# A decoder step on one core: the norm, the turning of x and the in-projection put into one block

## The chip, the cores and the metric

The kernel runs on one core of a Trainium2 chip. The metric is the device time of one execution in microseconds (us), lower is better. The core has five engines that run their own instruction streams and meet through semaphores: TensorE (PE, matmuls and transposes), VectorE (DVE), ScalarE (ACT), GpSimd (POOL) and SyncE (SP), which here issues all the DMAs.

## The reference, cut to what matters

All is float32. A prompt of 256 tokens and 8 samples of 4 tokens (288 tokens in all) pass one decoder layer with shared weights:

```python
h = rmsnorm(x, norm_mix)                      # 288 x 1024
proj = h @ w_in                               # 1024 x 3848: 1792 columns for RWKV, 2056 for the delta heads
xm = pr + (prev - pr) * mu_shift              # prev: the row before; for a sample's first row state_rwkv_shift
conv = sum(xp[:, j:j + t] * conv_w[j])        # xp: state_gdn_conv (3 rows) ahead of the projected rows
...                                           # RWKV7 and gated-delta recurrences, w_out, residual
x = x + cross_attention(rmsnorm(x), rmsnorm(mem, norm_mem))
x = x + routed_ffn(rmsnorm(x))                # top 4 of 32 experts, 12.6 MB of weights each
y = rmsnorm(x, final_norm)
```

The change touches only the start: `rmsnorm`, the transposed copy of `h`, the first of the projections and the small inputs that they need.

## The kernel before, in words

**Blocks.** The program is a row of blocks. In a block each engine has its own stream, written by hand; between two blocks all engines meet at a barrier. `front` holds two: a first one for the norm, and a second one for the projection and all that is computed from it. Then follow blocks for the recurrences, the read-out, the attention and the experts.

**The first block.** SP issues, in this order, the three parts of x (two of 128 tokens, one of 32: `TILES`), four norm vectors into `g8`, the weights of group 0 (`load_w(sp, 0)`), nine small vectors into the rows of `vrow`, the two states `shr` and `cvr` into `rc`, and the weights of group 1. ACT squares each part with a row sum (L358; the squares themselves go to `h_tm` and are overwritten) and takes the root (L361). DVE takes the reciprocal and scales the part into `h_tm` (L372, L373). PE turns it, 8 transposes a part (L394), one into each PSUM bank. When the third part is turned, DVE copies the even banks into `hT` and ACT the odd ones, times the norm vector (L378, L366). `idle_products` are products of the identity with itself into a bank that nobody reads, 18 of them at the start and 2 ahead of the second and of the third part; they keep PE at work while it would wait. POOL makes only `eps` and `ident` in this block.

**The second block.** PE first turns the small inputs (`turn_inputs`: `vrow` in one transpose, `shr` in 14, `cvr` in 12) into banks 0, 1 and 2, and DVE copies them into `vec`, `sprev` and `cprev`. Then come 31 projected tiles of 128 columns: `project(t)` is 8 products of 128 x 288 into bank 6 or 7 (an f32 product is two instructions). The weights come in groups of two tiles into three buffers, and a buffer's next load is issued when its last tile is projected. ACT empties a projected tile (`empty(t)`) after `turned_ok`, DVE mixes RWKV tiles (`mix(t)`), and between projections PE does the products that the mixed tiles call for (`decay` after tile 3, `rate` after 5, and so on). POOL builds the masks in this block; PE first waits for them in `key_squares`, after tile 7. SP's queue in this block starts with the weights of group 2, then six loads for `tail_in`, then a wait for `turned` and the load of `memx`, which lies over the columns of `rc` that held the states.

Of the kernel before, what the change touches and what calls it, by code (L numbers as in the profile page):

```python
# [19 lines left out]
P = 128  # L20
# [262 lines left out]
def front(nc, a, out, sb, ps, ident, ones, x, g8, eps, m):  # L283

    with ExitStack() as st:
# [9 lines left out]
        row, shr, cvr = rc[0:1 + NB, 0:R_PROJ], rc[0:NB, 0:R_PROJ], rc[0:NB * NJ, R_PROJ:]  # L295
# [13 lines left out]
        vec_in, small_in, tail_in = sem("vec_in"), sem("small_in"), sem("tail_in")  # L309
# [5 lines left out]
        def load_w(eng, g):  # L315
            c0, n = cols[g]
            eng.dma_start(wst[g % NG][:, :, 0:n], w_view[:, :, c0:c0 + n]).then_inc(w_in[g % NG], 16)

        with ExitStack() as s0:
            h_tm = sb(s0, "h_tm", [P, 3, D])  # L320
            x_sq, x_root, x_h, x_turned = (sem(n) for n in ("x_sq", "x_root", "x_h", "x_turned"))
            x_chain = Count(sem("x_chain"))
            with nc.Block() as block:
                @block.sync
                def _(sp):
                    xp = a["x_prompt"][0].rearrange("(i p) d -> i p d", p=P)
                    for i in range(2):
                        sp.dma_start(x[:, i, :], xp[i]).then_inc(x_in[i], 16)
                    sp.dma_start(x[:NS, 2, :], a["x_sample"].rearrange("b t d -> (b t) d")).then_inc(x_in[2], 16)
                    for i, n in enumerate(("norm_mix", "norm_cross", "norm_mem", "norm_ffn")):  # L330
                        sp.dma_start(g8[:, i, :], a[n][0].rearrange("(p c) -> p c", c=KC)).then_inc(small_in, 16)
                    load_w(sp, 0)
                    rows = [("mu_shift", V_MU, 14), ("a0", V_A0, 4), ("k_k", V_KK, 4), ("k_a", V_KA, 4),
                            ("r_k", V_RK, 4), ("lnx_w", V_LW, 4), ("lnx_b", V_LB, 4), ("conv_w", V_CW, 48),
                            ("gdn_norm_w", V_GN, 1)]
                    for name, r0, n in rows:
                        src = a[name][0]
                        src = (src.rearrange("h n -> (h n)") if name == "r_k" else
                               src.rearrange("w n -> (w n)") if name == "conv_w" else src)
                        sp.dma_start(vrow[r0:r0 + n, :], src.rearrange("(r p) -> r p", p=P)).then_inc(vec_in, 16)  # L340
                    sp.dma_start(shr, a["state_rwkv_shift"][0]).then_inc(vec_in, 16)
                    sp.dma_start(cvr, a["state_gdn_conv"][0].rearrange("b j n -> (b j) n")).then_inc(vec_in, 16)
                    load_w(sp, 1)

                @block.gpsimd
                def _(pool):
                    masks.step(pool, nc.gpsimd.memset(eps[:, 0:1], RMS_EPS))
                    masks.step(pool, nc.gpsimd.memset(eps[:, 1:2], GN_EPS))
                    masks.step(pool, nc.gpsimd.memset(ident[:], 1.0))
                    masks.step(pool, nc.gpsimd.affine_select(ident[:], ident[:], [[-1, P]], ALU.is_equal, 0.0, 0, 1))  # L350

                @block.scalar
                def _(act):
                    act.wait_ge(masks.sem, 1)
                    nc.scalar.activation(stat[:, 0, 3:4], eps[:, 0:1], ACT.Sqrt)
                    for i, (_, n) in enumerate(TILES):
                        act.wait_ge(x_in[i], 16)
                        nc.scalar.activation(h_tm[:n, i, :], x[:n, i, :], ACT.Square,  # L358
                                             accum_out=stat[:n, i, 0:1]).then_inc(x_sq, 1)
                        act.wait_ge(x_sq, i + 1)  # L360
                        nc.scalar.activation(stat[:n, i, 1:2], stat[:n, i, 0:1], ACT.Sqrt, bias=eps[:n, 0:1],  # L361
                                             scale=1.0 / D).then_inc(x_root, 1)
                    act.wait_ge(small_in, 64)
                    for c in range(1, KC, 2):
                        act.wait_ge(x_turned, c + 1)
                        nc.scalar.activation(hT[:, c, :], ps[:, c, 0:T], ACT.Copy, scale=g8[:, 0, c:c + 1])  # L366

                @block.vector
                def _(dve):
                    for i, (_, n) in enumerate(TILES):  # L370
                        dve.wait_ge(x_root, i + 1)
                        x_chain.step(dve, nc.vector.reciprocal(stat[:n, i, 2:3], stat[:n, i, 1:2]))  # L372
                        nc.vector.tensor_scalar(h_tm[:n, i, :], x[:n, i, :], stat[:n, i, 2:3], None,  # L373
                                                ALU.mult).then_inc(x_h, 1)
                    dve.wait_ge(small_in, 64)
                    for c in range(0, KC, 2):
                        dve.wait_ge(x_turned, c + 1)
                        nc.vector.tensor_scalar(hT[:, c, :], ps[:, c, 0:T], g8[:, 0, c:c + 1], None, ALU.mult)  # L378

                @block.tensor  # L380
                def _(pe):
                    pe.wait_ge(masks.sem, 4)

                    def idle_products(n):
                        for _ in range(n):
                            nc.tensor.matmul(ps[:, 7, 384:512], ident[:], ident[:], start=True, stop=True)

                    idle_products(18)
                    for i, (t0, n) in enumerate(TILES):
                        if i:  # L390
                            idle_products(2)
                        pe.wait_ge(x_h, i + 1)
                        for c in range(KC):
                            ins = nc.tensor.transpose(ps[:, c, t0:t0 + n], h_tm[:n, i, c::KC], ident[:n, :n])  # L394
                            if i == 2:
                                ins.then_inc(x_turned, 1)
# [43 lines left out]
        with nc.Block() as block:  # L440
            @block.sync
            def _(sp):
                load_w(sp, 2)
# [6 lines left out]
                sp.wait_ge(turned, 3)  # L450
# [17 lines left out]
            def _(pool):  # L468
                def keep(ap, pattern, base, cm):
                    masks.step(pool, nc.gpsimd.affine_select(ap, ap, pattern, ALU.is_ge, 0.0, base, cm))  # L470

                nc.gpsimd.memset(pr[:, :, 0:1], 0.0).then_inc(pads, 1)
# [46 lines left out]
            def _(pe):  # L519
                def project(t):  # L520
                    q = seq[t]
                    if t == 0 or seq[t - 1].group != q.group:
                        pe.wait_ge(w_in[q.group % NG], 16 * (q.group // NG + 1))
                    if t >= 2:
                        pe.wait_ge(ev, t - 1)
                    for c in range(KC):
                        ins = nc.tensor.matmul(ps[:q.n, 6 + t % 2, 0:T], wst[q.group % NG][:, c, q.at:q.at + q.n],  # L527
                                               hT[:, c, :], start=(c == 0), stop=(c == KC - 1))
                    ins.then_inc(prj, 1)

                def turn_inputs():
# [186 lines left out]
            def _(act):  # L718
# [34 lines left out]

                act.wait_ge(turned_ok, 3)
                for t in range(len(seq)):
# [54 lines left out]
                    elif t in (18, 20):  # L810
                        half = (t - 18) // 2
                        act.wait_ge(mem_t, half + 1)
                        for c in range(4 * half, 4 * half + 4):
# [47 lines left out]
            def _(dve):  # L861
# [44 lines left out]
                def products(which):  # L906

                    for name, j, f0, f1 in which:
# [3 lines left out]
                        for h in range(2):  # L912
# [4 lines left out]

                dve.wait_ge(turned, 1)
                nc.vector.tensor_copy(vec[:, :], ps[:, 0, 0:V_ROWS]).then_inc(turned_ok, 1)
                dve.wait_ge(turned, 2)  # L920
                nc.vector.tensor_copy(sprev[:, :, :].rearrange("p i b -> p (i b)"), ps[:, 1, 0:R_TILES * NB]).then_inc(
                    turned_ok, 1)
                dve.wait_ge(turned, 3)
                nc.vector.tensor_copy(cprev[:, :, :].rearrange("p i b -> p (i b)"),
                                      ps[:, 2, 0:C_TILES * NB * NJ]).then_inc(turned_ok, 1)
# [2282 lines left out]
```

## Time and the profile before

| | us |
|---|---|
| median of 3 runs | 1488.66 |
| lowest, highest run | 1487.46, 1493.93 |
| the profiled execution: span from first to last instruction | 1490.3 |
| PE busy in it | 1442.8 |

The profiled execution has no time of its own beside its span. Below, "busy" of PE is the time in which a matmul was under way, which is not the same as work at its peak. The granted clock is given as a share of 2.4 GHz: 1.00 is 2.4 GHz and 0.50 is 1.2 GHz. Times at the left of a row are from the span's start.

### The profile page before, as it was taken

To read this page: it belongs to the slowest core of one execution; us is meant where nothing else is said; L and a number is where in the kernel's file an instruction comes from. 1 tells how busy PE (TensorE), PEld (TensorE's weight loads), DVE (VectorE), ACT (ScalarE), POOL (GpSimd) and SP (SyncE) were. 2 spreads that over 40 slices of the span, in tenths; PEclk is the share of its full clock that TensorE was granted. 3 is DMA by queue.
4 is the path that set the end of the run, shared out by engine and by line. 5 is a ranking of instruction groups with operands and counts; after the bars stand their busy time and mean duration, and the time that the engine had idled before them with its cause. 6 is when DMAs were issued, how large, how long until landed. Compare 5 with 4: busy or idle time off the path is not lost.

```text
span 1490.3 us, 23019 instructions
## 1 busy us (share of the span) xinstructions
PE 1442.8 (97%) x9763; PEld 729.9 (49%) x9763; DVE 499.2 (33%) x994; ACT 216.8 (15%) x500; POOL 59.5 (4%) x103
## 2 busy tenths in 40 slices
PE   9999999999999999999999999999999999999996
PEld 7777788997477463333333333333333333333322
DVE  3585526237115043232242242223224223223213
ACT  3334222331114030000000000000000000000002
POOL 4010201310000000000000000000000000000000
PEclk9999999999999999999999999999999999999999
DMA  6233435105817667999999999999999999999993
GB/s 205 76 113 115 132 97 146 32 4 192 333 57 277 284 289 314 427 429 424 431 432 427 426 432 430 427 426 429 430 432 427 426 432 427 429 426 433 429 428 142
DMA packets 74693, 471.92 MB, mean 317 GB/s; under 512 B 14660, under 2 KB 48155, under 8 KB 58080
## 3 DMA queue, kind: packets, MB, share of 16 engines
q1 hardware_dynamic: 74592, 470.46, 77.0%
q8 instruction: 77, 1.26, 0.3%
q14 instruction: 24, 0.20, 0.0%
HBM read 463.40 MB, written 7.05 MB: 316 GB/s over the span
## 4 chain that ended last, share of the span: by engine, by line
PE 47%; DMA 16%; DVE 1%; ACT 0%; issue 0%; SPq 0%; DVEq 0%
PE ps L2811 22%; PE ps L2848 13%; DMA w<-in_w_e_dram 10%; PE ps L2596 3%; PE ps L2779 3%; DMA wb<-in_w_e_dram 3%; DMA wa<-in_w_e_dram 3%; PE ps L2803 2%; PE ps L2834 1%; PE ps L2600 1%; PE ps L2773 1%; PE ps L2839 1%; PE ps L2748 0%; PE ps L2756 0%; PE ps L2930 0%
## 5 line engine op out<-in xcount | busy, mean ns | idle before, releaser
L3029 DVE TENSOR_SCALAR kvb<-ps 128x512 f32<-128x512 f32 x32 | 22.1, 692 | 614.6 <-PE ps L2811 614.6
L2848 PE MATMUL ps<-w,kvb 128*64 128x512 f32 x640 | 143.1, 596 | 6.0 <-DMA w<-in_w_e_dram 6.0
L2811 PE MATMUL ps<-wb,kvb 128*64 128x512 f32 x480 | 107.5, 601 | 2.2 <-DMA wb<-in_w_e_dram 2.2
L2811 PE MATMUL ps<-wa,kvb 128*64 128x512 f32 x480 | 106.2, 595 | 2.4 <-DMA wa<-in_w_e_dram 2.4
L2811 PE MATMUL ps<-wc,kvb 128*64 128x512 f32 x448 | 100.8, 603 | 2.5 <-DMA wc<-in_w_e_dram 2.5
L2811 PE MATMUL ps<-wd,kvb 128*64 128x512 f32 x448 | 98.7, 593 | 0.0
L2980 ACT ACTIVATE kvb<-kvb 128x512 f32<-128x512 f32 x32 | 20.2, 631 | 499.0 <-DVE kvb L3029 499.0
L3013 DVE TENSOR_TENSOR x<-x,ps 128x1024 f32<-128x1024 f32 x66 | 79.9, 1216 | 32.7 <-PE ps L2779 32.6
L527 PE MATMUL ps<-yT,wkv 128*128 128x288 f32 x352 | 90.4, 415 | 0.0
L2848 PEld LDWEIGHTS ps<-w,kvb 128*64 128x64 f32 x640 | 43.6, 137 | 91.4 <-issue 79.1
L527 PEld LDWEIGHTS ps<-yT,wkv 128*128 128x128 f32 x352 | 67.2, 193 | 20.9 <-issue 2.7
L2779 PE MATMUL ps<-y,gT 64*128 64x512 f32 x264 | 73.4, 638 | 0.8 <-ACT y L2985 0.8
L2811 PEld LDWEIGHTS ps<-wb,kvb 128*64 128x64 f32 x480 | 34.4, 138 | 72.6 <-issue 69.4
L2811 PEld LDWEIGHTS ps<-wa,kvb 128*64 128x64 f32 x480 | 33.3, 137 | 74.1 <-issue 70.0
L2811 PEld LDWEIGHTS ps<-wc,kvb 128*64 128x64 f32 x448 | 31.5, 138 | 70.7 <-issue 67.3
L2596 PE MATMUL ps<-x,eh_tm 128*128 128x256 f32 x256 | 63.8, 392 | 0.3 <-DVE x L2611 0.3
L2811 PEld LDWEIGHTS ps<-wd,kvb 128*64 128x64 f32 x448 | 31.9, 137 | 64.7 <-issue 63.3
L1253 PE MATMUL ps<-wkv,hTm 128*128 128x256 f32 x256 | 57.1, 381 | 3.8 <-ACT kvb L1271 1.5
L2596 PEld LDWEIGHTS ps<-x,eh_tm 128*128 128x128 f32 x256 | 46.0, 189 | 27.6 <-issue 22.2
L2985 ACT ACTIVATE y<-ps 128x512 f32<-128x512 f32 x32 | 19.1, 597 | 246.9 <-PE ps L2848 246.9
L1253 PEld LDWEIGHTS ps<-wkv,hTm 128*128 128x128 f32 x256 | 48.0, 190 | 11.7 <-issue 5.4
L2811 PE MATMUL ps<-w,kvb 128*64 128x512 f32 x192 | 42.4, 594 | 0.6 <-DMA w<-in_w_e_dram 0.6
(647 smaller groups left out, 1706.9 us busy)
## 6 DMA issues: line engine op xcount, KB each, us to landing
w<-in_w_e_dram SPq DMA_DIRECT2D x40, 2048.0 KB, 23.3
wb<-in_w_e_dram SPq DMA_DIRECT2D x15, 4096.0 KB, 29.0
wa<-in_w_e_dram SPq DMA_DIRECT2D x15, 4096.0 KB
wc<-in_w_e_dram SPq DMA_DIRECT2D x14, 4096.0 KB, 27.2
wd<-in_w_e_dram SPq DMA_DIRECT2D x14, 4096.0 KB, 29.8
w<-in_w_e_dram SPq DMA_DIRECT2D x6, 4096.0 KB, 34.3
wa<-in_w_e_dram SPq DMA_DIRECT2D x6, 2048.0 KB, 30.6
wc<-in_w_e_dram SPq DMA_DIRECT2D x6, 2048.0 KB, 30.9
```

The source lines that it names most:

```text
L527: ins = nc.tensor.matmul(ps[:q.n, 6 + t % 2, 0:T], wst[q.group % NG][:, c, q.at:q.at + q.n], hT[:, c, :], start=(c == 0), stop=(c == KC - 1))
L1253: ins = self.nc.tensor.matmul(self.ps[:, 6, DX * i:DX * i + DX], self.hTm[:, c, P * i:P * i + P], self.w[:, n % self.NW, c, :], start=(c = ...
L2596: nc.tensor.matmul(ps[:, b + h, 0:4 * CAP], h_tm[:, i, P * (HK * h + c):P * (HK * h + c) + P], sel[:, i].rearrange("p e t -> p (e t)"), st ...
L2600: ins = nc.tensor.matmul(ps[m:m + CAP, b + j // 2, 0:4 * CAP], hs[r, c, :], sel[r, 2].rearrange("p e t -> p (e t)"), start=False, stop=Tru ...
L2779: ins = nc.tensor.matmul(ps[:, b + half, :], gT[r, i, :], y[r, :], start=True, stop=True)
L2803: ins = nc.tensor.matmul(ps[CAP * half:CAP * half + CAP, g, :], pick[r, half, :], b1[r, s % 2, :], start=True, stop=False)
L2811: ins = nc.tensor.matmul(ps[CAP * half:CAP * half + CAP, g, :], xe[:, h, c, :], wu[h][:, c, c0:c0 + 512], start=False, stop=(h == 1 and c ...
L2848: ins = nc.tensor.matmul(ps[CAP * half:CAP * half + CAP, 2, :], actT[:, c, h, :], wd[:, h, c, 512 * half:512 * half + 512], start=(h == 0 ...
L2980: nc.scalar.activation(th[:, :], hg[:, :], ACT.Tanh, scale=ALPHA / 2).then_inc(th_ok, 1)
L2985: nc.scalar.activation(y[:, :], ps[:, 2, :], ACT.Copy, scale=0.5).then_inc(y_ok, 1)
L3013: nc.vector.tensor_tensor(v, v, w, ALU.add).then_inc(add_ok if done is None else done, 1)
L3029: nc.vector.tensor_scalar(hg[:, :], ps[:, 0, :], LIMIT, None, ALU.min).then_inc(hg_ok, 1)
```

## The change

The first block is gone, and its streams stand at the head of those of the second. With that:

- SP issues the weights of group 0 ahead of the norm vector `norm_mix`; the other three norm vectors go behind the weights of group 1 (their reader, at tile 18, now waits for them itself). The weights of group 2 follow with no block boundary between.
- `h_tm` lies in `kvb` and the squares go to `junk` in `hTm`, so the block needs no memory of its own. The turned chunk c lands in bank (6 + c) % 8 in place of bank c.
- PE does 14 idle products in place of 18, and none between the parts. Tile 0 is projected right after the turning, each of its 8 products waiting for its own chunk of `hT` (`x_kept_by`). `turn_inputs` stands behind tile 0.
- `cvr` and `shr` are loaded under one another into the same columns of `rc` (rows 0 to 23 and 24 to 31), and 14 transposes of 32 rows turn both. POOL clears the 256 columns that `cvr` doesn't fill first, and SP waits for it.
- POOL's masks follow right behind `ident`.

The diff, cut to its core (what is moved without a change is left out):

```diff
-        row, shr, cvr = rc[0:1 + NB, 0:R_PROJ], rc[0:NB, 0:R_PROJ], rc[0:NB * NJ, R_PROJ:]
+        row = rc[0:1 + NB, 0:R_PROJ]
+        prev, cvr, shr = rc[0:NS, 0:R_PROJ], rc[0:NB * NJ, 0:CONV], rc[NB * NJ:NS, 0:R_PROJ]
+        h_tm = m.kvb[:, 0:3 * D].rearrange("p (i d) -> p i d", i=3)
...
-        with ExitStack() as s0:
-            h_tm = sb(s0, "h_tm", [P, 3, D])
...
-            with nc.Block() as block:
...
-                    idle_products(18)
-                    for i, (t0, n) in enumerate(TILES):
-                        if i:
-                            idle_products(2)
...
             def _(sp):
...
+                load_w(sp, 0)
+                sp.dma_start(g8[:, 0, :], a["norm_mix"][0].rearrange("(p c) -> p c", c=KC)).then_inc(mix_in, 16)
...
+                sp.dma_start(cvr, a["state_gdn_conv"][0].rearrange("b j n -> (b j) n")).then_inc(vec_in, 16)
+                sp.wait_ge(cleared, 1)
+                sp.dma_start(shr, a["state_rwkv_shift"][0]).then_inc(vec_in, 16)
+                load_w(sp, 1)
...
-                sp.wait_ge(turned, 3)
+                sp.wait_ge(turned, 2)
...
+                nc.gpsimd.memset(rc[0:NS, CONV:R_PROJ], 0.0).then_inc(cleared, 1)
...
                     for c in range(KC):
+                        if t == 0:
+                            pe.wait_ge(x_kept_by[c % 2], c // 2 + 1)
...
+                def turn_x():
+                    for i, (t0, n) in enumerate(TILES):
+                        pe.wait_ge(x_h, i + 1)
+                        for c in range(KC):
+                            ins = nc.tensor.transpose(ps[:, (6 + c) % 8, t0:t0 + n], h_tm[:n, i, c::KC], ident[:n, :n])
...
                 def turn_inputs():
+                    for done in x_kept_by:
+                        pe.wait_ge(done, KC // 2)
...
-                        ins = nc.tensor.transpose(ps[:, 1, i * NB:(i + 1) * NB], shr[:, i * P:(i + 1) * P],
-                                                  ident[:NB, :NB])
-                    ins.then_inc(turned, 1)
-                    for i in range(C_TILES):
-                        ins = nc.tensor.transpose(ps[:, 2, i * 24:(i + 1) * 24], cvr[:, i * P:(i + 1) * P],
-                                                  ident[:24, :24])
+                        ins = nc.tensor.transpose(ps[:, 1, i * NS:(i + 1) * NS], prev[:, i * P:(i + 1) * P],
+                                                  ident[:NS, :NS])
...
-                turn_inputs()
+                pe.wait_ge(masks.sem, 4)
+                idle_products(14)
+                turn_x()
                 for t in range(len(seq)):
                     project(t)
-                    if t == 3:
+                    if t == 0:
+                        turn_inputs()
+                    elif t == 3:
```

On PE, from the start of `front` on, there stood before (`ps` is PSUM, `ident` the identity, `yT` holds `hT`, `wkv` the weights of group 0; an x is a count):

```order
L386 MATMUL ps<-ident 128x128 x17
L394 MATMUL ps<-ident,h_tm 128x128 [waits in_x_h]
L394 MATMUL ps<-ident,h_tm 128x128 x7
L386 MATMUL ps<-ident 128x128 x2
L394 MATMUL ps<-ident,h_tm 128x32 [waits in_x_h]
L394 MATMUL ps<-ident,h_tm 128x32 x7
L323 UNCONDITIONAL_BRANCH
L518 UNCONDITIONAL_BRANCH [waits barrier_Pool_Activation_PE_DVE_SP_release]
L533 MATMUL ps<-ident,vrow 128x87 [waits in_vec_in]
L535 MATMUL ps<-ident,rc 128x8 x14
L539 MATMUL ps<-ident,rc 128x24 x12
L527 MATMUL ps<-yT,wkv 128x288 [waits in_w_in0]
```

And in the changed kernel, where `h_tm` shows as `kvb`:

```order
L486 MATMUL ps<-ident 128x128 x13
L492 MATMUL ps<-ident,kvb 128x128 [waits in_x_h]
L492 MATMUL ps<-ident,kvb 128x128 x7
L492 MATMUL ps<-ident,kvb 128x32 [waits in_x_h]
L492 MATMUL ps<-ident,kvb 128x32 x7
L480 MATMUL ps<-yT,wkv 128x288 [waits in_x_kept_v,in_w_in0]
L480 MATMUL ps<-yT,wkv 128x288 [waits in_x_kept_a]
L500 MATMUL ps<-ident,vrow 128x87 [waits in_vec_in,in_x_kept_a,in_x_kept_v]
L502 MATMUL ps<-ident,rc 128x32 x14
L480 MATMUL ps<-yT,wkv 128x288 x8
```

The barrier between the turned x and the projection is gone, tile 0 stands ahead of the small inputs, and these are 15 transposes in place of 27.

On SP, behind x, there stood before:

```order
L331 DMA g<-in_norm_mix_dram 128x8
L331 DMA g<-in_norm_cross_dram 128x8
L331 DMA g<-in_norm_mem_dram 128x8
L331 DMA g<-in_norm_ffn_dram 128x8
L317 DMA wkv<-in_w_in_dram 128x8x256
```

And in the changed kernel, where six of the nine rows that load `vrow` are left out, each of the others once:

```order
L322 DMA wkv<-in_w_in_dram 128x8x256
L374 DMA g<-in_norm_mix_dram 128x8
L382 DMA vrow<-in_mu_shift_dram 14x128
L382 DMA vrow<-in_conv_w_dram 48x128
L382 DMA vrow<-in_gdn_norm_w_dram 1x128
L383 DMA rc<-in_state_gdn_conv_dram 24x1536
L385 DMA rc<-in_state_rwkv_shift_dram 8x1792 [waits in_cleared]
L322 DMA stage_c<-in_w_in_dram 128x8x256
L388 DMA g<-in_norm_cross_dram 128x8
```

The first weights moved ahead of the norm vector, and three of the four norm vectors behind the second weights.

## Rows read from the trace of the kernel before

**Rows 1.** Page, parts 1 and 2: busy time, the DMA in 40 slices

```profile
PE 1442.8 (97%) x9763; PEld 729.9 (49%) x9763; DVE 499.2 (33%) x994; ACT 216.8 (15%) x500; POOL 59.5 (4%) x103
...
DMA  6233435105817667999999999999999999999993
```

**Rows 2.** Windows: us, busy time of each engine (rows touching it), TensorE's granted clock, DMA share

```profile
1.73:6.73 5.00, 5.00 (x23) 5.00 (x24) 0.82 (x2) 2.81 (x6) 0.00 (x0) 1.00 0.94 279
6.73:12.04 5.31, 5.31 (x47) 5.08 (x45) 2.56 (x7) 2.51 (x8) 0.00 (x0) 1.00 0.91 273
12.04:13.48 1.44, 0.01 (x1) 0.03 (x1) 1.14 (x3) 1.12 (x3) 0.03 (x1) 1.00 1.07 361
13.48:16.64 3.16, 3.15 (x27) 2.96 (x27) 0.52 (x2) 0.00 (x0) 2.59 (x11) 0.51 0.62 202
16.64:20.38 3.74, 3.74 (x9) 2.74 (x9) 1.75 (x8) 0.00 (x0) 3.13 (x10) 0.50 1.08 298
20.38:26.34 5.96, 5.96 (x26) 4.65 (x26) 2.90 (x15) 0.63 (x4) 5.06 (x14) 1.00 0.49 179
26.34:34.10 7.76, 7.76 (x34) 6.08 (x33) 2.68 (x7) 3.32 (x11) 5.04 (x19) 1.00 0.43 137
402.67:406.08 3.41, 3.13 (x16) 2.38 (x16) 1.98 (x4) 1.39 (x3) 0.00 (x0) 1.00 1.05 400
406.08:412.91 6.83, 6.15 (x14) 4.38 (x14) 0.00 (x0) 3.72 (x7) 0.00 (x0) 0.50 0.89 330
```

**Rows 3.** Timeline of TensorE (PE) from 0 to 140: start us, us, what

```profile
10.98 1.06 PE L394 MATMUL ps<-ident,h_tm 32*128 32x32 f32 x8
13.48 0.33 PE L533 MATMUL ps<-ident,vrow 87*128 87x87 f32 x1 [1.44 <-PEq L323]
13.75 1.66 PE L535 MATMUL ps<-ident,rc 8*128 8x8 f32 x14
15.26 1.45 PE L539 MATMUL ps<-ident,rc 24*128 24x24 f32 x12
16.64 9.86 PE L527 MATMUL ps<-yT,wkv 128*128 128x288 f32 x32
```

**Rows 4.** Timeline of 0 to 70: VectorE (DVE) and ScalarE (ACT) ahead of the projection

```profile
8.97 0.74 DVE L373 TENSOR_SCALAR h_tm<-x,stat 32x1024 f32<-32x1024 f32 x1
...
11.39 1.79 DVE L378 TENSOR_SCALAR yT<-ps,g 128x288 f32<-128x288 f32 x4 [1.68 <-PE ps L394]
11.49 1.68 ACT L366 ACTIVATE yT<-ps,g 128x288 f32<-128x288 f32 x4 [2.73 <-PE ps L394]
```

**Rows 5.** Same timeline: GpSimd (POOL), and one DVE line beside it and alone

```profile
13.45 0.11 POOL L472 MEMSET pr<- 128x4 f32 x1 [11.77 <-POOLq L323]
...
18.15 3.00 POOL L470 TENSOR_SCALAR_AFFINE_SELECT tr<-tr 128x128 f32<-128x128 f32 x7
...
32.23 0.31 POOL L505 MEMSET v_s<- 128x256 f32 x1
32.27 0.44 DVE L948 TENSOR_SCALAR rw<-xm,vec 128x288 f32<-128x288 f32 x1
...
36.14 0.37 DVE L948 TENSOR_SCALAR rw<-xm,vec 128x288 f32<-128x288 f32 x1
```

**Rows 6.** Same timeline: SyncE's DMA issues (SPq), and what waits for the last

```profile
4.07 0.67 SPq L317 DMA_DIRECT2D wkv<-in_w_in_dram  x1
...
17.61 0.43 SPq L449 DMA_DIRECT2D dtb<-in_a_log_dram  x1
...
22.94 0.24 DVE L937 COPY sc<-dtb 128x4 f32<-128x4 f32 x2 [4.33 <-DMA dtb<-in_a_log_dram]
```

**Rows 7.** DMA issues from 4 to 4.7: KB each, us from issue to landing

```profile
wkv<-in_w_in_dram SPq DMA_DIRECT2D x1, 1024.0 KB, 6.2
```

**Rows 8.** Timeline of SyncE, 493 to 600: experts' weights

```profile
567.41 0.35 SPq L2682 DMA_DIRECT2D wa<-in_w_e_dram  x1
```

**Rows 9.** Chain that ended last, 1340 to 1491: start us, us, what

```profile
1415.83 41.03 DMA wb<-in_w_e_dram
```

More of the change, by code:

```diff
@@ L308, in front @@
         x_in = [sem(f"x_in{i}") for i in range(3)]
-        vec_in, small_in, tail_in = sem("vec_in"), sem("small_in"), sem("tail_in")
+        vec_in, mix_in, small_in, tail_in = sem("vec_in"), sem("mix_in"), sem("small_in"), sem("tail_in")
+        x_sq, x_root, x_h, x_turned, cleared = (sem(n) for n in ("x_sq", "x_root", "x_h", "x_turned", "cleared"))
+        x_kept_by = [sem("x_kept_v"), sem("x_kept_a")]
+        x_chain = Count(sem("x_chain"))
         w_in = [sem(f"w_in{i}") for i in range(NG)]
@@ L529, in project, with idle_products @@
                     ins.then_inc(prj, 1)
+                def idle_products(n):
+                    for _ in range(n):
+                        nc.tensor.matmul(ps[:, 5, 384:512], ident[:], ident[:], start=True, stop=True)
+                def turn_x():
[3 more added lines that the diff above has]
+                            ins = nc.tensor.transpose(ps[:, (6 + c) % 8, t0:t0 + n], h_tm[:n, i, c::KC], ident[:n, :n])
+                            if i == 2:
+                                ins.then_inc(x_turned, 1)
                 def turn_inputs():
+                    for done in x_kept_by:
+                        pe.wait_ge(done, KC // 2)
                     pe.wait_ge(vec_in, 16 * 11)
@@ L752, in exps @@
                                              ACT.Exp, scale=s).then_inc(p_ready, 1)
+                act.wait_ge(masks.sem, 1)
+                nc.scalar.activation(stat[:, 0, 3:4], eps[:, 0:1], ACT.Sqrt)
+                for i, (_, n) in enumerate(TILES):
+                    act.wait_ge(x_in[i], 16)
+                    nc.scalar.activation(junk[:n, i % 2, :], x[:n, i, :], ACT.Square,
+                                         accum_out=stat[:n, i, 0:1]).then_inc(x_sq, 1)
+                    act.wait_ge(x_sq, i + 1)
+                    nc.scalar.activation(stat[:n, i, 1:2], stat[:n, i, 0:1], ACT.Sqrt, bias=eps[:n, 0:1],
+                                         scale=1.0 / D).then_inc(x_root, 1)
+                act.wait_ge(mix_in, 16)
+                for c in range(1, KC, 2):
+                    act.wait_ge(x_turned, c + 1)
+                    nc.scalar.activation(hT[:, c, :], ps[:, (6 + c) % 8, 0:T], ACT.Copy,
+                                         scale=g8[:, 0, c:c + 1]).then_inc(x_kept_by[1], 1)
                 act.wait_ge(turned_ok, 3)
@@ L916, in products @@
                                                     f1[r, :, TP:].rearrange("p (i j) t -> p i j t", i=2), ALU.mult)
+                for i, (_, n) in enumerate(TILES):
+                    dve.wait_ge(x_root, i + 1)
+                    x_chain.step(dve, nc.vector.reciprocal(stat[:n, i, 2:3], stat[:n, i, 1:2]))
+                    nc.vector.tensor_scalar(h_tm[:n, i, :], x[:n, i, :], stat[:n, i, 2:3], None, ALU.mult).then_inc(x_h, 1)
+                dve.wait_ge(mix_in, 16)
+                for c in range(0, KC, 2):
+                    dve.wait_ge(x_turned, c + 1)
+                    nc.vector.tensor_scalar(hT[:, c, :], ps[:, (6 + c) % 8, 0:T], g8[:, 0, c:c + 1], None,
+                                            ALU.mult).then_inc(x_kept_by[0], 1)
                 dve.wait_ge(turned, 1)
@@ L920, in _ @@
                 dve.wait_ge(turned, 2)
[L921 to L925, printed above, removed]
+                before = ps[:, 1, 0:R_TILES * NS].rearrange("p (i r) -> p i r", r=NS)
+                nc.vector.tensor_copy(sprev[:, :, :], before[:, :, NB * NJ:NS]).then_inc(turned_ok, 1)
+                nc.vector.tensor_copy(cprev[:, :, :], before[:, 0:C_TILES, 0:NB * NJ]).then_inc(turned_ok, 1)
                 dve.wait_ge(turned_ok, 3)
```

84 lines of the change are left out of this document (19 added, 65 removed).

## The prediction

> **What bounds the kernel now.** I read the page first, then the windows at the start, the timelines of the engines there, and last the chain that ended last. PE is busy for 1442.8 of 1490.3 us and the DMA engines are at nine tenths and more from the 16th slice of 40 on [rows 1]: the experts are bound by their weights, and the last wait of the chain is 41.03 us for such a load at 1415.83 [rows 9]. The change doesn't touch that. But the stream of weights isn't tied to the clock on the wall: its refills are issued as PE frees buffers, the first at 567.41 [rows 8]. If all that is ahead ends 5 us earlier, the stream starts and ends 5 us earlier. So the question is how much earlier PE comes out of the first blocks, and there PE is the engine to look at: from 13.48 on it has no gap up to 34.10 (busy 3.15 of 3.16, then 3.74 of 3.74, 5.96 of 5.96, 7.76 of 7.76) [rows 2]. I fix the point for the sum at the end of tile 1, which is 26.34 now.
>
> Before that point the reader should see four stretches on PE. Turning x ends at 10.98 + 1.06 = 12.04 [rows 3]. Then PE stands idle for 1.44 us until 13.48, while DVE and ACT copy the turned chunks (until 13.18 and 13.17 [rows 4]) and the barrier passes. The small inputs take from 13.48 to 16.64. Tiles 0 and 1 take 9.70 us from 16.64 to 26.34, where the next two tiles take 7.76, in 32 matmuls of 0.243 each. The difference is the clock: it was granted at 1.2 GHz from 13.5 to 20.38, right after the idle stretch, and at 2.4 GHz otherwise [rows 2].
>
> **The change part by part**, against the profiled execution's 1490.3.
>
> *Turning x earlier.* The third part is scaled at 8.97 + 0.74 = 9.71 [rows 4], but PE starts to turn it at 10.98 [rows 3], since 18 idle products, then two more, stand in the way. Of the idle matmuls 23 were under way in the first 5.00 us, 0.217 each; this is twice the later pace, so PE ran at the lower level there, though the column prints 1.00. With 28 in place of 36 they end near 6.73 + 5 x 0.11 = 7.3, before the second part is ready, and the third part is turned from 9.71 to 10.77 at the earliest. Gain 12.04 - 10.77 = 1.27.
>
> *No idle stretch.* The first copied chunk is there before 10.77: the first transpose of the part ends about 0.27 after 9.71 and a copy takes 1.79 / 4 = 0.45 [rows 4]. Two engines give two chunks each 0.45, and PE needs 4 x 0.243 = 0.97 for two, so `x_kept_by` never holds it after the first. Gain 1.44.
>
> *Small inputs.* Now: 3.16. A transpose of 8 rows costs (15.26 - 13.75) / 14 = 0.108, one of 24 rows (16.64 - 15.26) / 12 = 0.115 [rows 3]. One of 32 rows is the third part's: 8 in 1.06, with a tail, so 0.12. 14 x 0.12 + 0.27 = 1.95 for the new order. Gain 1.2. The wait for `x_kept_by` in it is long done.
>
> *Clock.* If PE stays at 2.4 GHz, tiles 0 and 1 take 7.76. Gain 9.70 - 7.76 = 1.94. This is the one uncertain large term. Its bounds: 1.94, and the other way a low stretch that falls wholly on projections costs 6.83 / 2 = 3.4, taking the length of the second one, 406.08 to 412.91 [rows 2], which turns the term to 1.94 - 3.4 = -1.5.
>
> *DVE beside POOL.* POOL was idle for 11.77 us ahead of 13.45; now the masks are built under the norm. The same DVE line took 0.44 beside a POOL memset and 0.37 alone [rows 5]: +0.07 is the near price. The upper bound is that each scaling waits out one of POOL's instructions, 3.00 / 7 = 0.43. Only the third scaling is on the path. I take -0.15, between the two and nearer to the row.
> The Trainium skill speaks against the change here: SBUF — State Buffer, section "Who interferes with whom", has it that a DVE `tensor_scalar` in a two-port mode and GpSimd share an exclusive port pair, and whoever comes second waits for the whole instruction. By that rule the sum would lose 0.43, not 0.15; the trace shows a slowdown of a fifth on one line and no full wait [rows 5].
>
> *DMAs.* Weights of group 0 took 6.2 us from issue at 4.07 [rows 6, 7], so landed at 10.3. They are now issued ahead of four norm vectors; even unmoved they are in time for 10.77. The norm vector that the copies need is issued just behind them, needed at 10; if it took as long as the weights, from about 3 on, it would land at 9.2. The small inputs were in by 13.48 and are needed at 10.77 + 3.9 = 14.7. Weights of group 2 and the six tail loads stood behind the barrier at 13.45; SP's queue now runs on into them, so the last of them, issued at 17.61 before, is issued some 4 us earlier, which covers most of the 4.33 us that DVE waited for it at 22.94 [rows 6]. What is queued behind the new wait for `cleared` (one state, all later loads) doesn't suffer: POOL clears 256 columns right after `ident`, long before SP gets there. I cost all of this at nothing; the cover on the weights is 0.5 us if they aren't earlier at all, and each us beyond it would cost one.
>
> *What is late next.* DVE begins to mix tile 0 some 3 us after the small inputs, which now stand behind tile 0 and not ahead of it. PE first needs a mixed tile in `decay`, after tile 3. It will be there 6 us earlier (28.3 for 34.10); DVE's wait of 4.33 shrinks in turn. I cost it at nothing, and it has some 3 us of room.
>
> Sum: 1.27 + 1.44 + 1.2 + 1.94 - 0.15 = 5.7. Span 1484.6. The profiled span lies 1.64 above the median of the three runs; I carry the difference over: 1488.66 - 5.7 = 1483.0, which is 0.38% less.
>
> **The rivals.** The measurement of this kernel tells about 0.5%, 7.4 us, from no change.
>
> 1. *The clock falls again, inside the turning or tile 0.* Turning is light work: from 402.67 to 406.08 PE did almost nothing but transposes (16, busy 3.13 of 3.41) and the clock was low in the stretch right after [rows 2]. The new order has 24 transposes from about 7.3 to 10.8 with two gaps (0.3 and 0.4 us) and no products between them, which the old order had. Against it: dense projection follows at once, not 1.44 us of nothing. Price 1.94 (as now) to 3.4: gain 3.8 to 2.3, time 1484.9 to 1486.4.
>
> 2. *More than the sum.* The low stretch from 406.08 to 412.91 cost about 6.15 / 2 = 3 us. It lies behind turning too, and nothing in the program fixes that it occurs; if the runs after are without it, or miss part of the loss at the end, the time is 1483.0 - 3 = 1480.
> TensorE: Matmul & The Clock Gate, section "What's actually happening" in the Trainium skill, says that the number of matmuls at the lower level at a kernel's start varies from run to run of one kernel. No row here can show it, there is one trace.
>
> 3. *Absorbed.* The start of the expert stream doesn't follow the start of the kernel, because a wait between 26 and 567 is set by something that isn't moved. The first refill follows a freed buffer [rows 8], which speaks against it. Gain 0 to 2, time about 1488.
>
> 4. *Slower.* Fewer idle products leave PE at 1.2 GHz through tiles 0 and 1: each matmul then takes twice 0.243 and the pair 15.5 us in place of 9.70. Against gains of 1.27 + 1.44 + 1.2 - 0.15 = 3.76 that is a loss of 5.8: time 1490.7. It decides from the point where over 3.76 / 0.243 = 15 more matmuls than now run low, which is all of a tile more. For it: the early rise needed 5 us of unbroken products, and there are now fewer. Against it: 28 of them still last to 7.3, past the rise at 6.7.
>
> **How the numbers follow.** Forecast (gain 4.5 to 7) 0.45; rival 1 0.28; rival 2 0.13; rival 3 0.09; rival 4 0.05. The predicted time is the forecast's, 1483.0. The range of 8 in 10 runs from 1480.3 (most of rival 2 with it) to 1488.2 (all of rival 1, half of 3). Faster by over 0.5% needs 1481.2 or less: rival 2 and the forecast's edge, 0.17. Slower by over 0.5% needs 1496.1, which no case here gives by itself; 0.03 is left for what I haven't seen. Within 0.5%: 0.80.
>
> **What would show it.** In the changed profile PE should turn the third part from about 9.8, start tile 0 within 0.2 us of its end, take 3.9 for it, 2.0 for the small inputs, and start tile 2 near 20.5. The clock column over 7 to 21 tells the forecast from rival 1. The first refill of `wa` should be issued near 561.7; if it isn't, rival 3 is right. A DVE scaling line over 1.1 us would show the port as dearer than I took it. The prediction is wrong if tile 0 waits for its weights, or if the blocks behind give the 6 us back.

## The result and the profile after

Both kernels ran 16 times: 1490.32 us median before, 1486.5 us after; ratio 0.9972, 95% interval 0.9961 to 0.9983. The change makes the kernel 0.28% faster, 0.17 to 0.39%. Run again beside the experiments it gave 0.9949 (0.993 to 0.9968) and 0.9969 (0.9955 to 0.9983). The profiled execution of after took 1484.06 us, span 1482.3; that of before had a span of 1490.3, and since a span is 1.76 us shorter than its time, it was one of 1492.1 us, 1.7 above the median. One run of before, beside e2, e4, e5 and e6, took 8317.95 us and counts in no ratio.

The timeline of PE in the kernel after (start us, us, what), which answers to [rows 3]:

```profile
1.72 6.27 PE L486 MATMUL ps<-ident 128*128 128x128 f32 x28 [1.72 <-POOL ident L421]
7.82 3.09 PE L492 MATMUL ps<-ident,kvb 128*128 128x128 f32 x24
10.92 4.12 PE L480 MATMUL ps<-yT,wkv 128*128 128x288 f32 x16
14.88 0.24 PE L500 MATMUL ps<-ident,vrow 87*128 87x87 f32 x1
15.05 1.05 PE L502 MATMUL ps<-ident,rc 32*128 32x32 f32 x14
16.02 4.15 PE L480 MATMUL ps<-yT,wkv 128*128 128x288 f32 x16
20.01 7.92 PE L480 MATMUL ps<-yT,stage_c 128*128 128x288 f32 x32
```

Its windows, which answer to [rows 2] (the clock is the third number from the end):

```profile
7.82:10.92 3.10, 3.00 (x26) 2.73 (x25) 2.19 (x5) 1.47 (x5) 2.76 (x6) 1.00 1.03 235
10.92:14.88 3.96, 3.96 (x17) 3.07 (x17) 1.13 (x3) 1.11 (x3) 3.33 (x10) 1.00 1.10 322
14.88:16.02 1.14, 1.14 (x16) 0.94 (x14) 0.25 (x1) 0.00 (x0) 1.00 (x3) 1.00 1.08 346
16.02:20.01 3.99, 3.99 (x19) 3.15 (x17) 1.87 (x9) 0.62 (x4) 3.13 (x14) 1.00 1.10 239
400.31:407.14 6.83, 6.15 (x15) 4.23 (x16) 0.52 (x1) 3.77 (x8) 0.00 (x0) 0.50 1.02 375
```

The reader should see that tile 2 starts at 20.01, where it started at 26.34: 6.33 us earlier, for a forecast of 5.7. Tile 0 starts as soon as the third part is turned, the idle stretch is gone, and so is the low stretch of the clock. The one at 400 is still there. SyncE's timeline and the chain that ended last show how the 6.33 travel, answering to [rows 8] and [rows 9]:

```profile
562.13 0.35 SPq L2671 DMA_DIRECT2D wa<-in_w_e_dram  x1
```

```profile
1410.27 40.35 DMA wb<-in_w_e_dram
...
1450.67 7.11 PE ps L2800 x32
```

The first refill is 5.28 earlier. The microsecond that is missing was lost in the recurrences: instruction by instruction, PE keeps its lead of 6.3 up to 273 us of before, and has 5.06 left from 309 on, where it waits for nothing that the profile names. That stretch scatters from execution to execution: in two more of the changed kernel it took 0.3 more than in before and 0.4 less. The work after the last weights begins at 1450.67 and not at 1456.91, 6.24 earlier: the wait for the last load began 5.56 earlier, and it was 0.68 shorter (40.35 for 41.03). In the chain of before that last group of 32 matmuls reads

```profile
1456.91 8.81 PE ps L2811 x32
```

and not 7.11; a low stretch fell into it. Only with those 1.7 us does the profiled pair differ by 8.0. This is chance and not the change's.

### The profile page after: what moved, and what is told of

Same layout as the page of the kernel before. It is cut to its first block, busy times and chain, and to the rows that moved or that the text cites. A ratio compares the mean times of both kernels' runs of the same rounds, so it can differ in the third digit from the quotient of the medians.

```text
span 1482.3 us, 22958 instructions
## 1 busy us (share of the span) xinstructions
PE 1437.0 (97%) x9735; PEld 725.4 (49%) x9735; DVE 498.4 (34%) x994; ACT 216.6 (15%) x500; POOL 60.9 (4%) x104
## 4 chain that ended last, share of the span: by engine, by line
PE 49%; DMA 14%; DVE 1%; ACT 0%; issue 0%; SPq 0%; DVEq 0%
PE ps L2800 23%; PE ps L2837 13%; DMA w<-in_w_e_dram 9%; PE ps L2585 4%; PE ps L2768 3%; DMA wb<-in_w_e_dram 3%; DMA wa<-in_w_e_dram 3%; PE ps L2792 2%; PE ps L2823 1%; PE ps L2589 1%; PE ps L2762 1%; PE ps L2828 1%; PE ps L2737 0%; PE ps L2745 0%; PE ps L2919 0%
```

## The experiments

Each is read in two ways: where tile 2 starts in its profile, and the time of its runs beside runs of before. Tile 2 is a good station because everything that the change touches lies ahead of it and the same work lies behind it in all kernels. All results together (the second column is the stretch up to 30 us in which PE's clock was below its full level):

```
                          tile 2 starts  PE clock low up to 30  median us  ratio to before  interval
before                    26.34          13.55 to 20.38
after                     20.01          no                     1486.5     0.9972           0.9961 to 0.9983
after, second time        20.52          no                     1485.03    0.9949           0.993 to 0.9968
after, third time         20.07          no                     1487.09    0.9969           0.9955 to 0.9983
e1 idle stretch filled    24.17          no                     1491.05    0.9996           0.9981 to 1.0011
e7 one block only         24.16          15.3 to 18.7           1491.13    0.9998           0.9981 to 1.0014
e3 inputs first           22.90          13.4 to 16.8           1487.87    0.9981           0.9966 to 0.9996
e8 loads+inputs first     22.64          13.6 to 17.0           1489.11    0.9983           0.9968 to 0.9997
e2 old idle products      21.41          no                     1487.54    0.9969           0.9952 to 0.9987
e4 two buffers            21.11          no                     1486.66    0.9972           0.9957 to 0.9987
e5 no idle products       20.98          no                     1488.77    0.9992           0.9979 to 1.0006
e6 masks later            20.03          no                     1485.24    0.9966           0.995 to 0.9982
e9 masks later, norm 1st  20.83          no                     1488.93    0.9975           0.996 to 0.999
```

The ratio of each row is to runs of before that ran beside it, interleaved. Those of before had medians from 1490.32 to 1491.41 us, so the medians of two rows are compared through their ratios and not directly.

### The idle stretch filled (e1)

```diff
+                    pe.wait_ge(x_first, 1)
+                    for _ in range(6):
+                        nc.tensor.matmul(ps[:, 0, 384:512], ident[:], ident[:], start=True, stop=True)
```

This stands in the kernel before, behind the turning; `x_first` says that bank 0 has been copied.

> The kernel before, with 6 idle products behind the turning of x, which end inside the wait of 1.44 us for the copies and the barrier (12.04 to 13.48). Nothing else is moved. Theory A, the clock falls because PE stands idle there: the clock stays at 2.4 GHz through the small inputs and tile 0, tiles 0 and 1 take 7.8 us and not 9.7, tile 2 starts at 24.4 and not 26.34, and the time falls by 0 to 2 us against before. Theory B, the clock falls because turning x is light work, whether idle time follows or not: it falls again between 10 and 17 and tile 2 starts at 26 or later.

Its timeline and windows of PE:

```profile
12.49 1.60 PE L401 MATMUL ps<-ident 128*128 128x128 f32 x12
14.39 0.27 PE L538 MATMUL ps<-ident,vrow 87*128 87x87 f32 x1 [0.30 <-PEq L323]
14.59 1.03 PE L540 MATMUL ps<-ident,rc 8*128 8x8 f32 x14
15.48 0.90 PE L544 MATMUL ps<-ident,rc 24*128 24x24 f32 x12
```

```profile
14.39:16.31 1.92, 1.91 (x28) 1.80 (x28) 0.52 (x2) 0.00 (x0) 1.52 (x8) 1.00 0.28 41
16.31:24.17 7.86, 7.86 (x34) 6.18 (x33) 3.11 (x14) 0.63 (x4) 6.63 (x19) 1.00 0.99 323
```

Theory A holds in this profile: no low stretch, tile 2 at 24.17, although the small inputs start 0.91 later than in before. And the trace shows something that I had missed: at 2.4 GHz the 27 transposes of the small inputs take 1.92 us and not 3.16. The time of the runs says nothing (0.9996; the 0.9987 that 2 us would give lies inside the interval); 2 us can't be told with 12 runs.

### One block and nothing else (e7)

The changed kernel with this undone: the 14 idle products, the one buffer and the order of tile 0.

```diff
-                idle_products(14)
+                idle_products(18)
                 turn_x()
+                turn_inputs()
                 for t in range(len(seq)):
                     project(t)
-                    if t == 0:
-                        turn_inputs()
```

> The changed kernel with all but the one block undone: 18 idle products and 2 between the parts, small inputs in two buffers and turned by 27 transposes ahead of tile 0. If the sum of the prediction holds, this has the idle stretch and the clock term alone: PE turns the third part from 11.0, starts on the small inputs at about 12.1 and tile 0 at 15.2, and tile 2 starts near 23.0 with the clock at 2.4 GHz (3.3 earlier than before). If the clock falls all the same, 24.5 to 25.

Timeline of DVE, ACT and PE, and the windows:

```profile
10.19 1.06 PE L491 MATMUL ps<-ident,kvb 32*128 32x32 f32 x8
...
10.87 1.68 ACT L735 ACTIVATE yT<-ps,g 128x288 f32<-128x288 f32 x4 [1.98 <-DMA g<-in_norm_mix_dram]
10.87 1.79 DVE L909 TENSOR_SCALAR yT<-ps,g 128x288 f32<-128x288 f32 x4 [0.98 <-DMA g<-in_norm_mix_dram]
...
12.70 0.27 PE L499 MATMUL ps<-ident,vrow 87*128 87x87 f32 x1 [1.45 <-DVE yT L909]
```

```profile
12.70:14.61 1.91, 1.91 (x27) 1.79 (x28) 0.52 (x2) 0.00 (x0) 1.68 (x4) 1.00 1.13 321
14.61:24.16 9.55, 9.55 (x34) 7.21 (x33) 3.31 (x21) 0.63 (x4) 5.77 (x21) 0.82 0.91 258
```

The barrier is gone and the idle stretch is as long as before: 1.45 us. The clock falls again. Tile 2 starts at 24.16, against an expected 23.0 (24.5 to 25 if the clock fell). Three things make up the 2.18 us against before. The small inputs start 0.78 earlier (12.70 for 13.48). They take 1.25 less (1.91 for 3.16) and tiles 0 and 1 take 0.15 less (9.55 for 9.70), both because the low stretch began at 15.3 and not at 13.55 and lasted 3.4 us and not 6.8. So leaving the barrier out is by itself worth 0.78 us of work at most; another wait comes to light behind it.

### The small inputs ahead of tile 0 (e3)

Of the changed kernel only the order is undone (the second part of the diff above; `turn_inputs` waits for the copies of banks 0 and 1).

> The changed kernel with the small inputs ahead of tile 0 (in one block, one buffer, 14 idle products). Theory A, the order of the two is worth nothing, since the first copies are there when the turning ends: tile 2 starts within 0.4 us of the changed kernel's 20.0, the time is the same. Theory B, projecting while the copies are still made hides something: tile 2 starts 0.5 to 1.5 later. A loss would also show if the small inputs weren't landed by 10.9.

```profile
9.93 1.06 PE L492 MATMUL ps<-ident,kvb 32*128 32x32 f32 x8 [0.26 <-DVE kvb L902]
...
10.33 1.79 DVE L906 TENSOR_SCALAR yT<-ps,g 128x288 f32<-128x288 f32 x4 [0.46 <-PE ps L492]
...
12.18 0.27 PE L500 MATMUL ps<-ident,vrow 87*128 87x87 f32 x1 [1.20 <-DVE yT L906]
12.38 1.04 PE L502 MATMUL ps<-ident,rc 32*128 32x32 f32 x14
```

```profile
12.18:13.35 1.17, 1.17 (x15) 1.04 (x15) 0.25 (x1) 0.00 (x0) 0.86 (x6) 1.00 1.11 344
13.35:22.90 9.55, 9.55 (x35) 7.28 (x33) 2.34 (x12) 0.63 (x4) 7.54 (x24) 0.82 1.02 282
```

Both theories fail: the order is worth 2.9 us of tile 2's start (22.90 for 20.01), more than the 0.5 to 1.5 of theory B. The last sentence of the expectation had named the case, inputs that haven't landed. Two things make it up: 1.20 us of idle time, and 9.55 us for tiles 0 and 1 in place of 7.95. The releaser in the row (DVE's last copy) is an inference, and `turn_inputs` waits here for the first two copies of each engine only. The semaphore events in the traces name another one: the last increment of the small inputs' load semaphore is at

```
before 12.48   after 11.90   e7 12.56   e3 12.05   e8 9.17   (us from the start)
```

and PE goes on within 0.13 us of it in e3 and e7 (12.15 and 12.67 on the weight-load side).

### Their loads first too (e8)

```diff
-                load_w(sp, 0)
...
                 sp.dma_start(shr, a["state_rwkv_shift"][0]).then_inc(vec_in, 16)
+                load_w(sp, 0)
                 load_w(sp, 1)
```

> The order inputs first once more, but now their loads are issued ahead of the weights of group 0 too. Theory A: in the run with the inputs first, PE stood idle until 12.15 because the small inputs had only landed at 12.05, and not because of the copies. Then here PE begins on the small inputs within 0.3 us of the end of the turning (near 11.0 or as soon as banks 0 and 1 are copied, 11.3), and the wait moves to the weights of group 0, which are now issued near 6.6 and land 6 to 8 us later: tile 0 starts at 12.6 to 14.5. Theory B: the copies set it; then PE again begins on the small inputs when DVE's last copy ends, near 12.1.

```profile
9.12 2.36 PE L492 MATMUL ps<-ident,kvb 128*128 128x128 f32 x16 [0.72 <-DVE kvb L902]
11.91 0.27 PE L500 MATMUL ps<-ident,vrow 87*128 87x87 f32 x1 [0.43 <-DVE yT L906]
```

```profile
13.09:22.64 9.55, 9.55 (x35) 7.21 (x33) 2.86 (x14) 0.63 (x4) 7.67 (x25) 0.82 1.08 327
```

DVE's copies ran here from 10.82 to 12.61, and PE went on at 11.91, long before their end: theory A. It went on 0.1 us after the second copy of either engine (11.76 and 11.81), and these free banks 0 and 1. So of the 1.20 us of e3 about 0.43 were these copies and the other 0.77 the landing. The weights of group 0 landed at 12.45 and held nothing up: tile 0 started at 13.09, right behind the inputs. But tile 2 is only 0.26 earlier for all this: x landed later in this execution, and the clock fell once more, with only 0.43 us of idle time ahead.

### The idle products as before (e2), and none (e5)

```diff
-                idle_products(14)
+                idle_products(18)
```

and two ahead of the second and third part in e2; `idle_products(0)` in e5.

> The changed kernel with the idle products of before: 18 at the start and 2 ahead of the second and third part. By the sum this undoes the first term alone: the third part is turned from 11.0 and tile 2 starts 1.1 to 1.3 later than the 20.0 of the changed kernel; time 1 us more if the clock is alike. Rival: the idle products held the clock up in more executions, and then the time is the same or less than the changed kernel's.

> The changed kernel without any idle product. This is the bound of rival 4 of the prediction: PE starts at 6.9 with the turning of x at the lower clock. If the clock rises only after some us of dense work, tile 0 and a part of tile 1 run at 0.485 us a product pair member in place of 0.243 and tile 2 starts 3 to 5 us later than 20.0. If it rises at once or is up already, no more than 1 us.

PE in e2, then in e5 (there with DVE's copies):

```profile
1.72 6.94 PE L486 MATMUL ps<-ident 128*128 128x128 f32 x36 [1.72 <-POOL ident L421]
...
11.25 1.06 PE L494 MATMUL ps<-ident,kvb 32*128 32x32 f32 x8
12.32 4.12 PE L480 MATMUL ps<-yT,wkv 128*128 128x288 f32 x16
```

```profile
7.04 4.66 PE L492 MATMUL ps<-ident,kvb 128*128 128x128 f32 x24 [7.04 <-POOL stri L416]
11.23 1.79 DVE L907 TENSOR_SCALAR yT<-ps,g 128x288 f32<-128x288 f32 x4 [1.30 <-DMA g<-in_norm_mix_dram]
11.90 4.12 PE L480 MATMUL ps<-yT,wkv 128*128 128x288 f32 x16 [0.20 <-DVE yT L907]
```

In e2 tile 0 starts at 12.32 for 10.92, tile 2 1.40 later: the first term, undone (1.1 to 1.3 expected; more on its size below). In e5 it is 0.97 later: here the transposes run at the lower clock and take 4.66 us for 24, but tile 0 takes 3.95 us as ever, from 11.90 on. So the clock was up before it, with no idle product in the program: its rise is recorded at 11.20, behind nothing but transposes. The copies began late too, since the norm vector landed only at 11.21; against the end of the turning at 11.70 that cost tile 0 at most the 0.20 us in its row. My expectation of 3 to 5 us was wrong, and rival 4 with it. Over its runs e5 gives away most of the gain, though (0.9992); one profile can't show whether the clock rises as early in each.

### Two buffers (e4)

The two states loaded side by side and turned by 14 and 12 transposes, as before, behind tile 0.

> The changed kernel with the two states in buffers of their own again, turned by 14 and 12 transposes behind tile 0. By the term in the sum (1.2 us) the small inputs take 3.1 us and not 2.0 or less on PE; tile 2 starts at 21.2 to 21.4. If transposes are bound by the clock and not by a floor, the difference is less, 0.7.

```profile
15.24 0.24 PE L497 MATMUL ps<-ident,vrow 87*128 87x87 f32 x1
15.41 1.03 PE L499 MATMUL ps<-ident,rc 8*128 8x8 f32 x14
16.30 0.90 PE L503 MATMUL ps<-ident,rc 24*128 24x24 f32 x12
17.13 4.15 PE L477 MATMUL ps<-yT,wkv 128*128 128x288 f32 x16
```

The small inputs take 17.13 - 15.24 = 1.89 us for 1.14 of the changed kernel: the buffer is worth 0.75, the lesser of the two values expected. The other 0.35 us by which tile 2 is later than in the changed kernel (21.11 for 20.01) lie ahead of it: the third part was scaled and turned later, and tile 0 starts at 11.29 for 10.92. A transpose of 8 rows costs (16.30 - 15.41) / 14 = 0.064, where [rows 3] gave 0.108, at the lower clock.

### POOL's masks held back (e6), and the norm vector first (e9)

```diff
+                pool.wait_ge(x_h, 3)
                 nc.gpsimd.memset(pr[:, :, 0:1], 0.0).then_inc(pads, 1)
```

and in e9 `norm_mix` ahead of `load_w(sp, 0)` as well.

> The changed kernel with POOL's masks held back until the third part is scaled, so that DVE has no neighbour while it scales. If POOL beside it costs DVE time, the third scaling takes 0.74 as in the kernel before and not 0.82, and tile 2 starts 0.1 earlier; the time is the same. If tile 2 doesn't move, the 0.08 wasn't on the path.

> The changed kernel with POOL's masks held back until x is scaled and with the norm vector issued ahead of the weights of group 0, which takes the two small lags of the changed kernel's traces: the third scaling at 0.74 in place of 0.82 to 1.07, and a norm vector that landed 0.3 us before the copies needed it. Expected: tile 2 starts at 19.9 to 20.1, 0 to 0.5 earlier than in the changed kernel; the time is the same within what 5 rounds tell.

The third scaling on DVE, in the second execution of after and in e6:

```profile
9.23 1.07 DVE L903 TENSOR_SCALAR kvb<-x,stat 32x1024 f32<-32x1024 f32 x1
```

```profile
9.08 0.74 DVE L904 TENSOR_SCALAR kvb<-x,stat 32x1024 f32<-32x1024 f32 x1
```

With the masks held back it takes 0.74 in both (e6, e9), with POOL at its masks 0.74 to 1.07 (0.82, 1.07 and 0.82 in the three of after; 0.79 in e7, 0.81 in e3, 0.74 in e8 and e5, 1.05 in e2 and e4). Tile 2 doesn't move in e6 (20.03, where 0.1 earlier was expected). The times of e6 and e9 are not told from those of the changed kernel. In e9 the parts of x landed late and tile 2 started at 20.83, so the expected 0 to 0.5 gain wasn't seen; neither is a version that beats the changed kernel.

### The changed kernel again (e0, e10)

> The changed kernel once more, beside the others on one chip. Mechanism: tile 2 starts at 20.0 when the clock stays up, as in its profile. If rival 1 of the prediction occurs in some executions, this profile or the spread of its granted clocks shows it: an execution with one more low stretch should be about 2 to 3 us longer, at a mean clock lower by 0.002.

> The changed kernel a third time, beside the two others. If the change is worth 3 to 4 us of work and the rest is the clock, then runs at the same mean granted clock differ by 3 to 4 us from before, and the mean clock is higher by 0.001 to 0.003. No low stretch between 7 and 21.

PE in the second execution:

```profile
8.71 1.15 PE L492 MATMUL ps<-ident,kvb 128*128 128x128 f32 x8 [0.62 <-DVE kvb L903]
10.36 1.06 PE L492 MATMUL ps<-ident,kvb 32*128 32x32 f32 x8 [0.49 <-DVE kvb L903]
11.43 4.12 PE L480 MATMUL ps<-yT,wkv 128*128 128x288 f32 x16
```

Here are the gaps between the parts that rival 1 feared, 0.62 and 0.49 (x landed later), and the clock stays up. With the mean granted clock of each run the time can be split. Each run is listed with its mean granted clock; these are the mean times of the runs at one clock, over the 59 runs of before beside the second and third time of after, and over all 35 of after (16, 8 and 11):

```
mean clock   0.990    0.991    0.992    0.993    0.994    0.995    0.996    all (us, clock)
before       1493.16  1491.75  1491.25  1489.49  1488.58                    1491.52  0.9915
after        1491.03  1488.70  1486.80  1486.82  1485.46  1484.54  1483.59  1486.15  0.9935
```

Within either row 0.001 of clock is worth 1.23 us (a straight line through both, with one slope). At one clock after is 2.9 us faster (standard error 0.25; 3.0 with the second and third time alone), just under the 3 to 4 expected. The rest of the 5.4, 2.4 us, goes with a clock that is 0.002 higher. The low stretch at the start that is gone makes just that much: 6.83 us at half the clock are 6.83 x 0.5 / 1490 = 0.0023 of the mean.

## Why the prediction was right, point by point

**Mechanism.** Forecast and result agree in sign and place, and nearly in size: 5.7 us forecast, 6.33 in the profiled pair up to tile 2, 5.4 between the means of the 35 runs of after and the 59 of before, 3.8 in the first medians. The forecast of the time itself was 1483.0, and the median is 1486.5. Of these 3.5 us, 1.7 come from the base (1488.66 in three runs, 1490.32 in sixteen) and 1.9 from the smaller gain in the medians. The number alone would have pointed to rival 1 (1484.9 to 1486.4, the clock falls again), and that didn't happen; the traces decide here, not the median. That 6.33 is so near 5.7 is in part luck, since two of the terms below hang on when the clock happens to change.

**Turning x earlier**, 1.27. The third part is done at 10.92 for 12.04: 1.1. Undone alone (e2), 1.4 of tile 2. Right for this pair. But the term depends on when the clock first rises, because the idle products run at half pace until then. With the same idle products the rise is recorded at 6.72 in before, 5.01 in e7, 7.33 in e2 and 7.81 in e1, and the third part is done at 12.04, 11.25, 12.31 and 12.56. Against 10.92 the term is 0.3 to 1.6. The prediction read one trace and took its rise for the rule.

**No idle stretch**, 1.44. Right in size, and right on what ended the stretch in the kernel before: the copies end 0.7 us after the small inputs had landed there (12.48). What was missing is the wait behind it. With the barrier gone and the order kept (e7), the copies that PE needs end at 12.23, the small inputs land at 12.56, and PE goes on at 12.70. So the block alone gives 0.78 of the 1.44. What removes the wait is that tile 0, whose weights are there (9.63), stands in front of them. In the prediction this was the sentence that the small inputs are needed at 14.7; it named the slack but not that without the new order the slack is negative.

**Small inputs**, 1.2: mis-sized. Measured 3.16 - 1.14 = 2.0. The step that failed is the 0.12 us for a transpose of 32 rows, 14 of which made up most of the 1.95 of the new order. It was read from the third part of x in [rows 3] (8 in 1.06, at 2.4 GHz by [rows 2]). The 14 transposes of the states have the same form in the profile and the same clock, and take 1.05 together. In e3, which shows both, they start 0.110 us apart in the third part (the row at 9.93) and 0.062 apart in the states (at 12.38). They differ in their reading and writing: x is read with every eighth column (`h_tm[:n, i, c::KC]`) and each transpose goes to another bank, the states are read with their columns side by side and go to one bank. Which of the two makes the price was not tried. The 0.108 and 0.115 for 8 and 24 rows, beside which 0.12 looked plausible, come from a stretch that [rows 2] shows at 1.2 GHz (0.51); at 2.4 they are 0.064 and 0.069 (e4). Of the 2.0, 0.75 are the buffer's (e4) and about 1.2 the clock's (e1: 1.92 for the same 27 transposes).

**Clock**, 1.94 on tiles 0 and 1: measured 9.70 - 7.95 = 1.75. Right. So the clock gave about 3.0 of the 6.33, and work and waiting the other 3.3; the runs at equal clock give 2.9 for these.

**DVE beside POOL**, -0.15: 0.08 in the profiled execution (0.82 for 0.74), up to 0.33 in others. The wait is seen better on the other side. In e7 and e4 POOL starts the mask `stri` ahead of DVE's scaling of the first part, in after behind its start (the scaling runs from 6.07 to 6.82 in e7 and after). POOL's row in e7, then in after:

```profile
5.95 0.29 POOL L414 TENSOR_SCALAR_AFFINE_SELECT stri<-stri 128x128 f32<-128x128 f32 x1
```

```profile
6.19 0.78 POOL L416 TENSOR_SCALAR_AFFINE_SELECT stri<-stri 128x128 f32<-128x128 f32 x1
```

The same instruction takes 0.29 us where it comes first and 0.78 in after, where it ends at 6.97, 0.15 behind DVE's scaling. In e0, e2 and e3 it is 0.84, 0.77 and 0.82. That is what one sees if POOL waits out DVE's instruction. DVE's third scaling, the other way round, took 0.31 to 0.33 longer in three of nine profiles (e0, e2, e4). The Trainium skill, page SBUF — State Buffer, section "Who interferes with whom", states an exclusive lock between these two engines' ports; the 0.49 that POOL loses here agree with it.

**Rivals.** *The clock falls again*: given 0.28. Between the turning and tile 2 it never did in the changed kernel's three profiles nor in the five variants with tile 0 in front of the inputs (e2, e4, e5, e6, e9); of a run without a profile this can't be said. It fell in all three in which light work or waiting went on behind the turning (e7, e3, e8), and in before. So "against it", dense projection follows at once, was the stronger argument. *More than the sum*: the low stretch at 400 stayed in the profiles of after. *Absorbed*: the first refill is 5.28 earlier, so no (561.7 forecast, 562.13 measured). *Slower*: e5 answers it; in its profile even without idle products tile 2 loses only 1 us.

**Left open.** e7 starts tile 2 2.2 us earlier than before and its runs aren't faster (0.9998). The interval reaches to 0.9981, which holds 2.2 us, so nothing contradicts; and of the 2.2 only 0.78 were work, the rest was where its low stretch fell. The same line, fitted to the runs of one experiment and those of before beside it, gives the difference from before at equal clock: e7 0.3 us slower (standard error 0.4), e5 0.6 faster (0.5), e3 1.7 (0.5), e4 2.0 (0.3), e2 2.5 (0.3). So the block alone shows nothing in the runs. Why e5 loses more in its runs than in its profile wasn't tried. Nor was why PE takes up to 1.6 us more for the recurrences between 273 and 309 in one execution of the changed kernel than in another.

## What to carry to other kernels

Put the product that only needs the big, early load first, and the small inputs behind it: many small transfers in one queue with megabyte loads land late, and with dense work right behind the transposes TensorE's clock stayed up here in 8 of 8 profiles. Before taking a duration from a row, look at the clock of that stretch, and whether the instruction reads and writes in the same pattern as the one that you want to price: 0.12 and 0.07 us were the prices of one form here. When a change moves a few microseconds in 1500, read it at a station in the trace, and compare runs at equal mean clock; the medians alone gave anything from 3.8 to 6.4 us for one and the same change.

## What the runs showed of the hardware

- Short waits among transposes went with a fall of the clock: in e8 only 0.43 us of idle time lay ahead of the low stretch of 13.6 to 17.0, between the transposes of x and those of the inputs. Transposes alone didn't bring it down: in the changed kernel 3.1 us of them, followed by dense products, left it up, and in e5 it rose at 11.20 behind 4.2 us of nothing else. Six idle products in 1.44 us kept it up too (e1).
- With idle products from 1.72 on, the clock's first rise is recorded between 5.01 and 7.81 us in twelve profiles.
- Each of the 13 profiled executions has a low stretch between 400 and 414, where x is turned too. Others come and go: one or two of 3.4 us between 147 and 172 in seven of them, each worth 1.7 us of PE's lead, and one of 10.2 to 13.7 us between 524 and 544 in three (e0, e1, e4), worth 3.9 to 5.4. The mean clock of a run varied from 0.986 to 0.997, and 0.001 of it went with 1.23 us.
- A norm vector of 4 KB landed 4.4 to 5.4 us after its issue when it stood ahead of the first weights (before, e1, e8, e9), and 6.8 to 8.3 us when it stood behind them; in e7 and e5 both copying engines waited for it.
- The clock column prints 1.00 until the first change in an execution, also where matmuls run at half pace (28 in 6.10 us from 1.72 to 7.82 in the kernel after).
